# A streaming encoder layer: decay rows without block diagonals, other distances between the steps, and the convolution's pairs in another order

## The chip, the cores and the metric

One Trainium2 chip, one of its cores. The metric is the device time of one execution in microseconds (us), the median of three runs. The engines are TensorE (PE, with its weight loads as PEld), VectorE (DVE), ScalarE (ACT), GpSimd (POOL) and the queue of SyncE (SP), from which the weights are loaded.

## The reference, cut to what matters

One layer of an encoder over 512 prompt frames and 32 further frames of a running stream, all in fp32, with the same weights:

```python
h = rmsnorm(x, g1)
z = h @ w_in                       # 1024 -> 8200 columns, split:
(mq, mk, mv, mo, mi, mf, sb, sc, sx, dq, dk, dv, gt) = jnp.split(z, splits, axis=-1)
# A) mLSTM, 4 heads of 128: per block w = exp(dlog - m), inter = exp(a - m)
s = einsum(q, k) * w
num = einsum(s, v) + inter * einsum(q, C)          # den likewise; C, n carried on
ya = sigmoid(mo) * rmsnorm(num / den, ml_g)
# B) short convolution of width 3
yb = sb * causal_dwconv(sc * sx, hist, sc_w)
# C) differential attention, 4 heads, block-causal mask in chunks of 64
yc = rmsnorm(einsum(softmax(q1 k1) - lam * softmax(q2 k2), v), da_g)
x = x + (sum over branches of sigmoid(gt) * (y_branch @ w_br)) @ w_o
x = x + (silu(conv(up1)) * conv(up2)) @ w_dn       # ConvFFN, width 2816
y = rmsnorm(x, norm_f)
```

The further frames attend to 1024 cached keys as well and start from a given mLSTM state. The outputs are y and the states of both groups.

## The kernel before

Activations stand transposed, channels in the partitions and the 544 frames in the free dimension. Each fp32 product is made of three fp32r matmuls on split operands (high by high, low by high, high by low). The input projection runs over *pairs* of 2 x 128 output columns with a Strassen scheme: seven products ("blocks", `p(pair, w)`, w = 1 to 7) of 4 x 3 = 12 matmuls of 272 columns each, L1677 in `strassen_product`. Other products (branches `pr`, `wo`, `up`, `dn`) are L1645. ACT makes the high part of each weight unit (w_h, L978) and DVE the low part (w_l, L1260), four units ahead of PE; DVE also makes the Strassen weight sums (tw, L1275) and drains three of seven blocks (L1406), ACT the other four (L1093).

All engines run through one list, ORDER, each picking its steps. A planner writes it: `put` and `project` add blocks, and each calls `tick`, a clock that counts one for a block and two for a branch product. `at_time(time, step)` notes a step with its due time, and `tick` puts it into the list once the clock has come to it. So a distance in due times is a distance in blocks of PE. Four chains are placed so:

- The mLSTM, five units u (the 32 further frames first, then four tiles of 128), t0 = 32 + 8u. `s`: PE's decay exponents and scores (L1789 to L1796); `w`: ACT's exponential; `pt`, `qi`: DVE's products (L1464, L1459); `kw`: POOL's product (L845); `n`: PE's numerators (L1809 to L1812), which wait for pt, qi and kw; `rd`, `sq`, `rr`, `hn`: the norm on DVE, ACT, POOL, DVE; `h`: PE's transposes (L1819), which wait for hn; `hm`: ACT's copy; `bd`: POOL's block diagonals for the next unit.
- The decay rows. dlog - m is a column term plus a row term u for each head. The row term and the factor inter are spread over the partitions by one matmul each, with the constant mean_r as stationary operand over 36 rows: `bd_u` and `bd_i` [36, 4, L] hold for each head its row in its own column block, once as high and once (rows 32 to 35) as low part. `block_diagonal` makes them on POOL (L796) from `ui`, which DVE fills in rows step 2.
- The sample group: cached keys (`ck`), then for each of two maps scores (`s`, L1848), maximum (`mx`, DVE) and exponential (`ex`, ACT, L1176).
- Attention, units 1 to 16 (4 heads by 128, 256, 384 and 512 keys), one each 7 due times; unit 0 is the sample group's rest. `s`: scores of both maps (L1862) and the mask (L1867); `mx`; `ex` (L1187); `wd`: DVE's difference of the softmaxes (L1294); `t`: PE's transposes of it (L1882); `wt`; `o` (L1899); `sq`, `rr`, `on`, `y`, `yt`, `yc`: norm and split. The mask adds a product of a row of `causal` (NEG in its first 64 columns) with a row of `mean_r` to the last 64 keys.

The steps that follow a pair (`post`) are due from the clock at which its last block was put: for sx, u0 and u1 (DVE's products of sc and sx, L1534), w0 and w1 (ACT), c0 and c1 (DVE's two sums, L1546 and L1548); for sb, y, hi and lo (L1556, ACT, L1521).

At the start ACT squares the rows of x for the first norm (L955). At the end the last norm needs the sum of squares over the eight column blocks: `mean_square` part 0 over the first seven, part 1 over the last (L1692), then DVE's sum, POOL's power (L912) and the scaling of four prompt chunks and the further frames' rows, each followed by its store.

## Time and profile before

| | us |
|---|---|
| median of 3 runs | 1035.94 (1034.19 to 1041.75) |
| the profiled execution | 1035.7 |
| its span | 1033.9 |
| PE busy | 984.5 |
| DVE busy | 694.6 |
| ACT busy | 462.2 |
| POOL busy | 161.3 |

Durations below come from the one profiled execution; 1.8 us of its time lie outside the span. Matmuls overlap in the pipeline, so the duration of a row with one matmul is longer than the distance to the next start. PEclk is the granted clock of TensorE as a share of 2.4 GHz. "<-" names what a wait ended with; "issue" is a wait for which the profile shows nothing.

### The profile page before, as it was taken

To read this page: it belongs to the slowest core of one execution; us is meant where nothing else is said; L and a number is where in the kernel's file an instruction comes from. 1 tells how busy PE (TensorE), PEld (TensorE's weight loads), DVE (VectorE), ACT (ScalarE), POOL (GpSimd) and SP (SyncE) were. 2 spreads that over 40 slices of the span, in tenths; PEclk is the share of its full clock that TensorE was granted. 3 is DMA by queue.
4 is the path that set the end of the run, shared out by engine and by line. 5 is a ranking of instruction groups with operands and counts; after the bars stand their busy time and mean duration, and the time that the engine had idled before them with its cause. 6 is when DMAs were issued, how large, how long until landed. Compare 5 with 4: busy or idle time off the path is not lost.

```text
span 1033.9 us, 19957 instructions
## 1 busy us (share of the span) xinstructions
PE 984.5 (95%) x7714; PEld 953.9 (92%) x7714; DVE 694.6 (67%) x1176; ACT 462.2 (45%) x965; POOL 161.3 (16%) x348
## 2 busy tenths in 40 slices
PE   6999998998999988899999999999999999999996
PEld 4999887997999987799999999999999999999996
DVE  6887656768666687777787556777777777634342
ACT  5665454465555545555454433433343334322221
POOL 2010222210111111012012211221212121111010
PEclk8999999999999999999999999999999999999998
DMA  6523242364232222232245222222222223423212
...
DMA packets 98069, 96.98 MB, mean 94 GB/s; under 512 B 4740, under 2 KB 93721, under 8 KB 97719
## 3 DMA queue, kind: packets, MB, share of 16 engines
...
## 4 chain that ended last, share of the span: by engine, by line
PE 80%; DVE 9%; ACT 5%; issue 4%; POOL 1%; DMA 0%; ACTq 0%; DVEq 0%; POOLq 0%
PE D L1645 43%; PE D L1677 26%; PE D L1662 2%; DVE w_l L1260 2%; ACT w_h L978 1%; PE X L1862 1%; DVE tw L1275 1%; PE X L1899 1%; DVE ups L1601 1%; DVE acc L1611 1%; PE X L1809 1%; ACT tmp L1150 1%; PE X L1810 1%; PE X L1867 1%; ACT tmp L955 1%
## 5 line engine op out<-in xcount | busy, mean ns | idle before, releaser
L1260 DVE TENSOR_TENSOR w_l<-raw,w_h 128x512 fp32r<-128x512 f32 (+1 forms) x274 | 194.8, 729 | 131.2 <-ACT w_h L978 124.7
L1677 PE MATMUL D<-a_h,w_h 128*128 128x272 f32 x840 | 252.8, 301 | 10.3 <-DVE tmp L1406 5.1
L1677 PE MATMUL D<-a_h,w_l 128*128 128x272 f32 x840 | 245.4, 292 | 0.0
L1677 PE MATMUL D<-a_l,w_h 128*128 128x272 f32 x840 | 244.1, 291 | 0.0
L978 ACT ACTIVATE w_h<-raw 128x512 fp32r<-128x512 f32 (+1 forms) x274 | 163.4, 619 | 105.5 <-PE D L1645 77.2
L1677 PEld LDWEIGHTS D<-a_h,w_h 128*128 128x128 f32 x840 | 160.3, 191 | 15.2 <-DVE tmp L1406 6.5
L1677 PEld LDWEIGHTS D<-a_l,w_h 128*128 128x128 f32 x840 | 160.8, 191 | 0.0
L1677 PEld LDWEIGHTS D<-a_h,w_l 128*128 128x128 f32 x840 | 160.3, 191 | 0.0
L1645 PE MATMUL D<-h_h,w_h 128*128 128x272 f32 x704 | 146.0, 289 | 0.0
L1645 PE MATMUL D<-h_h,w_l 128*128 128x272 f32 x704 | 145.8, 289 | 0.0
L1645 PE MATMUL D<-h_l,w_h 128*128 128x272 f32 x704 | 145.2, 288 | 0.0
L1260 DVE TENSOR_TENSOR w_l<-tw,w_h 128x512 fp32r<-128x512 f32 x120 | 83.9, 707 | 47.0 <-ACT w_h L978 41.5
L1645 PEld LDWEIGHTS D<-h_h,w_h 128*128 128x128 f32 x704 | 110.7, 188 | 0.2
L1645 PEld LDWEIGHTS D<-h_l,w_h 128*128 128x128 f32 x704 | 110.7, 189 | 0.0
L1645 PEld LDWEIGHTS D<-h_h,w_l 128*128 128x128 f32 x704 | 109.9, 189 | 0.0
L1223 ACT ACTIVATE acc<-ups,fcw 128x546 f32<-128x546 f32 x44 | 33.1, 753 | 162.6 <-POOL ffn_last L922 162.6
L978 ACT ACTIVATE w_h<-tw 128x512 fp32r<-128x512 f32 x120 | 75.4, 628 | 67.2 <-PE D L1677 27.0
L1645 PE MATMUL D<-g_h,w_h 128*128 128x272 f32 x352 | 73.4, 290 | 0.7 <-DVE w_l L1260 0.7
L1604 DVE SCALAR_TENSOR_TENSOR acc<-ups,fcw,acc 128x546 f32<-128x546 f32 x44 | 34.7, 788 | 57.8 <-ACT acc L1223 57.8
L1645 PE MATMUL D<-g_l,w_h 128*128 128x272 f32 x352 | 72.8, 288 | 0.0
L1645 PE MATMUL D<-g_h,w_l 128*128 128x272 f32 x352 | 72.7, 288 | 0.0
L1645 PEld LDWEIGHTS D<-g_h,w_h 128*128 128x128 f32 x352 | 55.2, 189 | 1.3 <-DVE w_l L1260 1.0
...
## 6 DMA issues: line engine op xcount, KB each, us to landing
...
xT<-x_spill ACTq DMA_DIRECT2D x1, 2176.0 KB, 11.5
```

Of the source, the lines that this page charges most:

```text
L955: sc.activation(tmp[0:L].rearrange("p a b -> p (a b)")[:, 0:DM], x_t[:, c, :] if c < 4 else x_s[0:TS, :], ACT.Square, accum_out=ssx[0:L, c ...
L978: sc.activation(split_view(w_h, g), whole_view(g), ACT.Copy).then_inc(S["wh_ready"], 1)
L1150: last = sc.activation(ml_junk[0:L, P * h:P * h + P], X[0:L, h // 2, 129 * (h % 2):129 * (h % 2) + P], ACT.Square, scale=rden[0:L, h:h + 1 ...
L1223: sc.activation(acc[part][:, j % 2, 0:T + 2], ups[m % 2][:, 2:T + 4], ACT.Copy, scale=fcw[:, 2, jj:jj + 1])\
L1260: v.tensor_tensor(split_view(w_l, g), whole_view(g), split_view(w_h, g).bitcast(F32), ALU.subtract)\
L1275: v.tensor_tensor(t_view(q, w), x, y, op).then_inc(S["t_ready"], 1)
L1601: last = v.tensor_tensor(to, d, r, ALU.mult)
L1604: link(v.scalar_tensor_tensor(out=ac, in0=u[:, 1:T + 3], scalar=fcw[:, 1, jj:jj + 1], in1=ac, op0=ALU.mult, op1=ALU.add))
L1611: v.scalar_tensor_tensor(out=s[:, 0:T + 2], in0=tmp[:, tmp_row[("up", j)], 0:T + 2], scalar=1.0, in1=s[:, 0:T + 2], op0=ALU.add, op1=ALU.m ...
L1645: last = t.matmul(banks(n)[:, half, 0:HALF], w[:, k, :], x[:, kx + k, HALF * half:HALF * half + HALF], start=kx + k == 0 and i == 0, stop= ...
L1662: last = t.matmul(banks(n)[0:w.shape[2], half, 0:HALF], w[:, k, :], left_of(x, kx)[:, half, :], start=kx == 0 and i == 0, stop=kx == KD - ...
L1677: last = t.matmul(out, wt[:, k, :], x[:, left, k, :], start=w in (1, 2, 5) and k == i == 0, stop=k == KQ - 1 and i == 2, skip_group_check= ...
```

## The change

- Pairs: the convolution's come as sc 0, sx 0, sc 1, sx 1, sb 0, sb 1 (before sc 0, sc 1, sx 0, sx 1, sb 0, sb 1). Its later post steps are due one or two blocks later.
- mLSTM units: every 9 due times (before 8), h at 8.9 (7.9), hm and the state's store at 10 (9). The bd step is gone.
- Decay rows: `sel` is a [4, 4] identity in fp32. For each head one fp32 matmul spreads the row u (added to the causal term) and one the row inter, with a column of sel, repeated, as stationary operand: 4 + 4 matmuls in place of two, without bd_u, bd_i and their POOL and DVE steps. The scores come last.
- Sample group: keys' load due 72 (before 68), transposes 81 and 83 (77, 79), map 0 at 85 to 87 (81 to 83), map 1 at 90 to 92 (84 to 86).
- Attention: starts at 99 (94), the distance to the next unit is 5, 6, 7, 10 after 128, 256, 384, 512 keys (before 7); y, yt and yc keep their distance to the next unit's o.
- Mask: a matrix `late_half` with NEG in row 0 and row 64, so that each map's mask works on its own 64 rows, in fp32; POOL writes it behind the store of C_p.
- Start: ACT squares a constant into `kap` ahead of the first wait for x.
- End: the mean of the first seven blocks (`mean`) and the last one (`norm`) are apart, with the transposes of the last block between; DVE scales chunks 0 to 2, ACT chunk 3 and the further frames' rows.

```diff
-    pairs += [(s, jj) for s in ("sc", "sx", "sb") for jj in range(2)]
+    pairs += [("sc", 0), ("sx", 0), ("sc", 1), ("sx", 1), ("sb", 0), ("sb", 1)]
...
-        t0 = 32 + 8 * u
-        for dt, sub in ((0, "s"), (1, "w"), (1, "qi"), (2, "pt"), (2, "kw"), (3, "bd"), (4, "n"), (5, "rd"), (6, "sq"),
-                        (6, "c"), (6, "rr"), (7, "hn"), (7.9, "h"), (9, "hm")):
-            if sub != "bd" or u < 4:
-                at_time(t0 + dt, "ml", sub, u)
+        t0 = 32 + 9 * u
+        for dt, sub in ((0, "s"), (1, "w"), (1, "qi"), (2, "pt"), (2, "kw"), (4, "n"), (5, "rd"), (6, "sq"),
+                        (6, "c"), (6, "rr"), (7, "hn"), (8.9, "h"), (10, "hm")):
+            at_time(t0 + dt, "ml", sub, u)
         if ML_ORDER[u] >= 3:
-            at_time(t0 + 9, "ml", "out", u)
-    at_time(68, "ck_load")
-    for time, step in ((72, ("ck", 0)), (74, ("ck", 1)), (76, ("sample", "s", 0)), (77, ("sample", "mx", 0)),
-                       (78, ("sample", "ex", 0)), (79, ("sample", "s", 1)), (80, ("sample", "mx", 1)),
-                       (81, ("sample", "ex", 1))):
-        at_time(time + 5, *step)
+            at_time(t0 + 10, "ml", "out", u)
+    at_time(72, "ck_load")
+    for time, step in ((81, ("ck", 0)), (83, ("ck", 1)), (85, ("sample", "s", 0)), (86, ("sample", "mx", 0)),
+                       (87, ("sample", "ex", 0)), (90, ("sample", "s", 1)), (91, ("sample", "mx", 1)),
+                       (92, ("sample", "ex", 1))):
+        at_time(time, *step)
     for u in range(17):
-        t0 = 94 + 7 * (u - 1) - (u == 0)
+        t0, t1 = (99 + 28 * (x // 4) + (0, 5, 11, 18)[x % 4] if x >= 0 else 91 for x in (u - 1, u))
         for dt, sub in ((0, "s"), (1, "mx"), (2, "ex"), (3, "wd"), (5.5, "t"), (6.5, "wt"), (8, "o"), (9, "sq"),
-                        (9, "rr"), (11.5, "on"), (15, "y"), (16, "yt"), (16, "yc")):
+                        (9, "rr"), (11.5, "on"), (t1 - t0 + 8, "y"), (t1 - t0 + 9, "yt"), (t1 - t0 + 9, "yc")):
             if u or dt > 2:
                 at_time(t0 + dt, "at", sub, u)
...
-                                  (1, "sx", "u0"), (2, "sx", "w0"), (3, "sx", "c0"), (3, "sx", "u1"),
-                                  (4, "sx", "w1"), (5, "sx", "c1"), (1, "sb", "y"), (2, "sb", "hi"), (3, "sb", "lo")):
+                                  (1, "sx", "u0"), (2, "sx", "w0"), (3, "sx", "c0"), (5, "sx", "u1"),
+                                  (6, "sx", "w1"), (7, "sx", "c1"), (1, "sb", "y"), (3, "sb", "hi"), (5, "sb", "lo")):
...
+    unit("mean")
+    unit("yT", KD - 1)
     unit("norm", 2)
-    unit("yT", KD - 1)
     unit("scale")
...
+        sel = place("sel", [H, H])
...
+        ui = at(33632, "ui", [H, 2, T])
+        row["u"], row["inter"] = ui[:, 0, :], ui[:, 1, :]
...
+        ml_junk = at(37984, "ml_junk", [P, H * P])
...
+        late_half = at(41472, "late_half", [P, P])
...
+            for c in range(3):
+                sp.wait_ge(S["y_dve"], c + 1)
                 sp.dma_start(y_p[0, P * c:P * c + P, :], yst[:, c, :]).then_inc(S["y_out"], 16)
-            sp.wait_ge(S["y_dve"], 3)
-            sp.dma_start(y_s[0], yst_s[0:TS, :]).then_inc(S["y_out"], 16)
...
-            g.affine_select(out=sel[0:H], in_=sel[0:H], compare_op=ALU.not_equal, fill=float(DM), base=0,
+            g.affine_select(out=sel[:], in_=sel[:], compare_op=ALU.not_equal, fill=1.0, base=0,
                             pattern=[[-1, H]], channel_multiplier=1).then_inc(S["const_ready"], 1)
...
-            def block_diagonal(u):
-                col, L = TILES[ML_ORDER[u]]
-                if u >= 1:
-                    pool.wait_ge(S["ml_scores"], u)
-                for i, out in enumerate((bd_u, bd_i)):
-                    last = g.tensor_tensor(out[:, :, 0:L],
-                                           ui[:, i, col:col + L].bitcast(F32).unsqueeze(1).to_broadcast([36, H, L]),
-                                           sel[:].unsqueeze(2).to_broadcast([36, H, L]), ALU.mult)
-                last.then_inc(S["bd_ready"], 1)
...
-                elif kind == "ml" and a[0] == "bd":
-                    block_diagonal(a[1] + 1)
...
-                    pool.wait_ge(S["ui_ready"], 1)
-                    block_diagonal(0)
...
+                elif kind == "sample" and a == ("ex", 0):
+                    pool.wait_ge(S["out_C"], 64)
+                    link(g.memset(late_half[:], 0.0))
+                    link(g.memset(late_half[0:1, 0:64], NEG))
+                    g.memset(late_half[64:65, 0:64], NEG).then_inc(S["mask_ready"], 1)
+                    pool.wait_ge(S["mask_ready"], 1)
...
+            sc.activation(kap[:], m_half[:], ACT.Square)
...
+                    sc.activation(yst[:, 3, :], yst[:, 3, :], ACT.Copy, scale=ssx[:, 3:4]).then_inc(S["y_act"], 1)
+                    act.wait_ge(S["y_act"], 1)
+                    act.dma_start(y_p[0, 3 * P:4 * P, :], yst[:, 3, :]).then_inc(S["y_out"], 16)
+                    sc.activation(yst_s[0:TS], yst_s[0:TS], ACT.Copy, scale=ssx[0:TS, 4:5]).then_inc(S["y_act"], 1)
+                    act.wait_ge(S["y_act"], 2)
+                    act.dma_start(y_s[0], yst_s[0:TS, :]).then_inc(S["y_out"], 16)
...
-                        .then_inc(S["rows_act"], 1)
+                        .then_inc(S["rows_act"], 2)
...
+
+                    r = 2 if kind == "mean" else a[0]
...
-                    for c in (0, 2):
+                    for c in range(3):
                         v.tensor_scalar(yst[:, c, :], yst[:, c, :], ssx[:, c:c + 1], None, ALU.mult)\
                             .then_inc(S["y_dve"], 1)
-                    v.tensor_scalar(yst_s[0:TS], yst_s[0:TS], ssx[0:TS, 4:5], None, ALU.mult)\
-                        .then_inc(S["y_dve"], 1)
...
-                    dve.wait_ge(S["rows_dve"], 6)
-                    v.memset(ui[:].bitcast(F32), 0.0)
-                    link(v.tensor_copy(sel[32:36], sel[0:H]))
-                elif kind == "rows" and a[0] == 2:
-
-                    dve.wait_ge(S["rows_act"], 2)
-                    v.tensor_copy(ui[0:H, 0, :], row["u"])
-                    link(v.tensor_copy(ui[0:H, 1, :], row["inter"]))
-                    for i, nm in enumerate(("u", "inter")):
-                        last = v.tensor_tensor(ui[32:36, i, :], row[nm], ui[0:H, i, :].bitcast(F32), ALU.subtract)
-                    last.then_inc(S["ui_ready"], 1)
...
-                        B = banks(block_of[("dn", KD - 2)])
-                        wait_drained(pe, block_of[("dn", KD - 2)])
-                        for part in range(2):
-                            mean_square(2, part, B[:, part, 0:5])
+                        mean_square(2, 1, banks(block_of[("dn", KD - 2)])[:, 1, 0:5])
+                elif kind == "mean":
+                    wait_drained(pe, block_of[("dn", KD - 2)])
+                    mean_square(2, 0, banks(block_of[("dn", KD - 2)])[:, 0, 0:5])
...
+                            pe.wait_ge(S["rows_act"], 3)
                             for i in range(4, 8):
                                 wait_drained(pe, last_user[i])
                         else:
                             pe.wait_ge(S["ml_c"], u)
 
-                        pe.wait_ge(S["bd_ready"], u + 1)
-                        lw, inter = (X[:, i, :].rearrange("p (h t) -> p h t", h=H)[:, :, 0:L] for i in (0, 2))
+                        lw = X[:, 0, :].rearrange("p (h t) -> p h t", h=H)[:, :, 0:L]
                         t.matmul(lw[0:L], ident_r[0:L, 0:L], causal[0:L, 0:L].unsqueeze(1).to_broadcast([L, H, L]),
                                  start=True, stop=False, skip_group_check=True)
-                        t.matmul(lw[0:L], mean_r[0:36, 0:L], bd_u[:, :, 0:L], start=False, stop=True,
-                                 skip_group_check=True)
                         for h in hs:
-                            t.matmul(X[0:L, 1, P * h:P * h + L], mkT[:, h, col:col + L], mqT[:, h, col:col + L],
+                            t.matmul(X[0:L, 0, P * h:P * h + L], sel[:, h:h + 1].to_broadcast([H, L]), row["u"][:, col:col + L],
+                                     start=False, stop=True, skip_group_check=True)
+                        for h in hs:
+                            t.matmul(X[:, 2, P * h:P * h + L], sel[:, h:h + 1].to_broadcast([H, P]), row["inter"][:, col:col + L],
                                      start=True, stop=True)
-                        t.matmul(inter, mean_r[0:36, :], bd_i[:, :, 0:L], start=True, stop=True)\
-                            .then_inc(S["ml_scores"], 1)
+                        for h in hs:
+                            last = t.matmul(X[0:L, 1, P * h:P * h + L], mkT[:, h, col:col + L],
+                                            mqT[:, h, col:col + L], start=True, stop=True)
+                        last.then_inc(S["ml_scores"], 1)
...
+                            pe.wait_ge(S["mask_ready"], 1)
...
+                            d = slice(64 * c, 64 * c + 64)
+                            last = t.matmul(X[:, c, nk - 64:nk], late_half[d, :], mean_w[d, 0:64], start=False,
                                             stop=True, skip_group_check=True)
                         last.then_inc(S["at_s"], 1)
```

## Rows read from the trace of the kernel before

**Rows 1.** The page, busy time: engine, us (share of the span), instructions.
```profile
PE 984.5 (95%) x7714; PEld 953.9 (92%) x7714; DVE 694.6 (67%) x1176; ACT 462.2 (45%) x965; POOL 161.3 (16%) x348
```

**Rows 2.** Waits of PE, whole span: us in total, times, longest.
```profile
PE X L1882 <- DVE prob L1294: 5.7, 4, 1.9
PE X L1819 <- DVE qi L1487: 5.6, 5, 1.4
...
PE D L1677 <- DVE tmp L1406: 5.1, 6, 1.2
...
PE X L1809 <- issue: 3.0, 1, 3.0
PE X L1848 <- ACT prob L1176: 2.1, 1, 2.1
...
PE D L1677 <- ACT tmp L1093: 1.5, 3, 1.0
```

**Rows 3.** Windows: stretch, length; busy of PE, PEld, DVE, ACT, POOL; PEclk; DMA; GB/s.
```profile
118.00:236.00 118.00, 107.23 (x814) 100.25 (x813) 77.19 (x145) 59.28 (x163) 27.44 (x37) 0.97 0.41 112
330.00:440.00 110.00, 98.90 (x710) 91.34 (x709) 83.33 (x162) 59.68 (x149) 14.62 (x43) 0.95 0.25 68
440.00:560.00 120.00, 119.39 (x938) 116.95 (x937) 89.97 (x146) 65.39 (x140) 18.43 (x32) 1.00 0.32 95
```

**Rows 4.** Windows of two short stretches, columns as in rows 3.
```profile
118.30:119.50 1.20, 1.20 (x6) 1.14 (x6) 0.00 (x0) 0.00 (x0) 0.00 (x0) 0.50 0.05 14
162.00:165.20 3.20, 3.12 (x14) 3.15 (x15) 3.20 (x6) 0.50 (x1) 0.00 (x0) 0.50 0.00 0
```

**Rows 5.** Timeline of PE, scores of unit 1: start, us, engine, line, operation.
```profile
128.24 0.49 PE L1791 MATMUL X<-bd_u,mean_w 36*128 36x512 f32 x1
128.66 1.16 PE L1794 MATMUL X<-mqT,mkT 128*128 128x128 f32 x8
129.75 0.50 PE L1796 MATMUL X<-bd_i,mean_w 36*128 36x512 f32 x1
```

**Rows 6.** Timeline of PE, the first tile's kw products.
```profile
116.94 1.50 PE L1812 MATMUL X<-mv_tok,kw 32*128 32x129 f32 x8
```

**Rows 7.** Timeline of DVE and POOL ahead of unit 2's numerators.
```profile
157.00 4.03 DVE L1275 TENSOR_TENSOR tw<-raw,tw 128x512 f32<-128x512 f32 x1
...
158.44 1.04 POOL L796 TENSOR_TENSOR bd_u<-ui,sel 36x512 fp32r<-36x512 f32 x1
...
161.31 0.67 DVE L1464 TENSOR_TENSOR p_ml<-w_ml,X 128x512 f32<-128x512 f32 x1
```

**Rows 8.** Timeline of DVE and PE around the transposes of attention unit 9.
```profile
375.96 0.78 DVE L1546 SCALAR_TENSOR_TENSOR scb<-u_c,vec,scb 128x546 f32<-128x546 f32 x1
...
377.62 0.65 DVE L1534 TENSOR_TENSOR u_c<-tmp,scb 128x480 f32<-128x480 f32 x1
...
378.96 0.35 DVE L1294 SCALAR_TENSOR_TENSOR prob<-prob,kap 128x128 f32<-128x128 f32 x1
...
379.37 0.33 PE L1882 MATMUL X<-ident,prob 128*128 128x128 f32 x1 [1.59 <-DVE prob L1294]
```

**Rows 9.** Timeline of PE, scores and mask of attention unit 8.
```profile
352.46 1.13 PE L1862 MATMUL X<-dkT,dqT 64*128 64x512 f32 x4
...
353.52 0.41 PE L1867 MATMUL X<-mean_w,causal 1*128 1x64 f32 x2
```

**Rows 10.** Timeline of ACT and PE at the start.
```profile
5.08 1.28 ACT L955 ACT_TABLE_LOAD   x1 [5.08 <-DMA x_t<-in_x_prompt]
...
13.74 0.41 PE L1698 MATMUL X<-diag,mean_w 32*128 32x32 f32 x2 [0.28 <-DVE diag L1327]
```

**Rows 11.** Timeline of PE at the end.
```profile
1022.27 1.21 PE L1692 MATMUL D<-mean_w,tmp 128*128 128x1 f32 x10
...
1023.40 0.66 PE L1919 MATMUL X<-ident,xT 128*128 128x128 f32 x4
```

**Rows 12.** The chain that ended last: one block of 12 matmuls, start and us.
```profile
111.10 1.51 PE D L1677 x12
```

38 lines of the change are left out of this document (13 added, 25 removed).

## The prediction

> **What bounds the kernel now.** I read the page's busy line first: TensorE (PE) is busy 984.5 us, 95% of the span [rows 1]. A change that leaves PE's own work alone can give back only PE's idle stretches and the time at the lower clock. So I asked the waits of PE next [rows 2], and a table by stage to see where they lie [rows 3]. From 118 to 236 us (the mLSTM units) PE idles 118 - 107.23 = 10.8 us; from 330 to 440 us (the short convolution with attention) 110 - 98.90 = 11.1 us; from 440 to 560 us, with the same attention but no convolution, only 0.6 us. The reader is to see in that table also the granted clock, 0.97 and 0.95 of full where PE idles, 1.00 where it doesn't. Short windows show the two levels: 0.50 (1.2 GHz) from 118.3 and from 162.0 us [rows 4]; the second follows an idle of 3 us [rows 2], the first no idle but matmuls with few rows or columns, those of [rows 6] last. At half clock a stretch costs half its length.
>
> **Decay rows (PE work added).** A full unit loses two fp32r matmuls over 512 columns, which start 0.42 us (128.24 to 128.66) and some 0.43 us ahead of what follows: 0.85 us [rows 5]. It gains eight fp32 matmuls of 4 rows by 128 columns, each two passes: 16 passes. The nearest passes of that width with 128 rows are the scores, eight passes in 1.09 us, 0.136 us each [rows 5]; the nearest with few rows are those with kw of the first tile, eight in about 1.45 us (1.50 with their drain), 0.18 us each, part of it at half clock [rows 6]. The mask's one-row passes are worse still: 0.17 us for 64 columns, and 64 more columns are an eighth of a 512-column pass, 0.53 / 8 = 0.07: 0.24 us [rows 9]. Bounds: 16 x 0.136 - 0.85 = +1.3 us and 16 x 0.24 - 0.85 = +3.0 us a unit. I take 0.155 us, close to the kw row less what is clock in it, since those are fp32 passes in a run of their own as the new ones are: 16 x 0.155 - 0.85 = +1.63 us, four units +6.5 us. The first tile has 32 columns; its price lies between 0 and that of a full unit, I take +1.0. Sum +7.5 us, bounds +5.2 and +13.5.
>
> The Trainium skill speaks against the change here. "TensorE: Matmul & The Clock Gate", Part 3, says a weight load overlaps a running matmul only when its row group differs, and its LDWEIGHTS section gives 128 columns as 128/1.2 = 107 ns. By it each pass is a load and then a stream of about the same length, 0.21 us, an estimate that would make the item some 12 us; the trace has no pass of 4 rows by 128 columns to say so.
>
> **Clock behind them.** The half clock from 118.3 us came after matmuls that fill little of the array [rows 4, 6]. A unit now has 2.5 us of 4-row matmuls ahead of its scores. A stretch at half clock costs half its length, about 1 us for one of the size of that from 118.3 to 121 us. Bounds 0 and five of them; I take one: +1.0 us.
>
> **Spacing 9 and h later.** The transposes of h wait five times for hn, 5.6 us in all, 1.4 at most [rows 2]. Step h now stands one more block (1.51 us of PE work [rows 12]) behind hn, and a block covers the longest of them: -5.6 us. The 3.0 us wait in front of unit 2's numerators [rows 2] is one of DVE: a tw sum that begins at 157.00 lasts 4.03 us while POOL runs kw, bd_u and bd_i, so p_ml ends only at 162.0 [rows 7]. The two bd products a unit (1.04 us each) are removed, and kw stands three blocks behind the store that it followed directly. Both go: -3.0 us, and with it the half clock from 162.0 to 165.2, half of 3.2 = -1.5 us [rows 4]. Sum -10.1 us. If a wait of about 1 us comes up between tok drains and the shifted units, -9.
>
> **Sample group.** The second scores wait 2.1 us for the first exponential [rows 2], three blocks after the first scores; they now stand five blocks after. -2.1 us. PE's 1.5 us for ACT's tmp drains comes while ACT waits for a maximum in the same stretch; the distance from maximum to exponential is unchanged, so I take half: -0.8 us. Bounds for both together: 0 and -3.6.
>
> The first attention output (o of unit 0) moves from ahead of pr(0, 0) to behind it in the order, and DVE, which must wait for at_o before it drains pr(0, 0), is held for as long as PE takes for a group of transposes, a block and o. PE has four split units (6 us) in hand and needs that drain only for pr(0, 1), which stands behind o, s and one more block. Nothing, or +1 us if DVE catches up late.
>
> **Mask.** Per unit two one-row fp32r matmuls over 64 columns take 0.34 us between starts (0.41 with their drain) [rows 9]. Their successors have two passes each, but lie in different row halves. If the halves overlap, as two maps of 512 columns in 1.06 us suggest [rows 9] (four passes, each four times the columns of a 0.136 us pass, would be 2.2 one after the other), the price is the same; if not it is up to 0.15 us more. 16 units: I take -0.3, bounds -2 and +2.4 us.
>
> **Convolution order and spacing.** DVE did two conv sums c0 (the first at 375.96, 0.78 us each) and the product u1 (0.65 us and small ones) between the exponential and the softmax difference (378.96); PE's transpose waits from 377.8 to 379.37 [rows 8]. The same pattern stands at units 9 to 12: prob 5.7 us in four waits, the drains that come late after them 5.1 us in six [rows 2], and stretches at half clock behind three of them. The table's 0.95 over 110 us caps that loss at 5.5 us [rows 3]; ten matmuls at double interval in each make it 3. In the new order sx 0 stands one pair (7 blocks) earlier, u1 and c1 two blocks later, y, hi and lo are spread, and attention takes 5, 6, 7, 10 blocks for 128 to 512 keys rather than 7 each. By the due times, unit 9's difference then has only u0 ahead of it, unit 10's only u1. So the waits should go. But DVE is full: 83.3 us in this stretch [rows 3], where PE without idle and slow clock needs 110 - 11.1 - 3 = 96 us: it would have to be busy 87% of it, in order and without a wait that PE feels. I count on two thirds of 11.1 + 3 = 14.1 us: -9 us, bounds -3 and -13.
>
> **Start and end.** ACT's table load (1.28 us at 5.08, behind the first data) moves ahead of the data, but PE waits only 0.28 us for the last diag that depends on it [rows 10]; DVE's copies hold the rest. -0.4 us, bounds 0 and -1.3. At the end the last column block's transposes (0.7 us) move ahead of the last mean square, which ran 1022.27 to 1023.40 [rows 11]; POOL's power and both scalings follow 0.7 us later, and the DVE now has three chunks. The store of y_s is shorter than the chunk issued last before, which gives a little back. +0.7 us, bounds -0.5 and +1.5.
>
> **Sum.** +7.5 + 1.0 - 10.1 - 2.9 - 0.3 - 9.0 - 0.4 + 0.7 = -13.5 us. The profiled execution took 1035.7 us (span 1033.9 and 1.8 around it), the median of three is 1035.94: 1035.7 - 13.5 = 1022.2, say 1022 us.
>
> **Rivals.**
> (A) DVE's load, not its order, bounds the convolution: the idle moves by 7 blocks and shrinks by 2 to 3 us only. For it: 83.3 us busy with PE stalled. Against: DVE idles 110 - 83.3 = 26.7 us of the same stretch. 1022 + 6.5 = 1028.5 us. Chance 0.17.
> (B) In the 4-row passes weight load and stream don't overlap: 0.18 to 0.24 us a pass, by the kw and the mask rows, +9.5 to +13.5 for the item, in the middle +11.5: 1026 us. For it: both rows have few array rows. Against: part of the one is half clock, the other is fp32r between streams of another shape. 0.20. This is what the page's rule above would make.
> (C) Slower: the eight 4-row matmuls a unit lower the clock and it doesn't come back between units. Place: the five units. Work at half clock takes twice its time. The units span 5 x 9 blocks of 1.51 us, 68 us of work; with a fifth of it (13.5 us) at half clock the gain is gone, with half of it the time is 1022 + 34 = 1056 us. For it: [rows 4]'s fall without idle. Against: the blocks between the units gave the clock back there before the next unit. 0.05.
> (D) The change's waits do go but come up elsewhere in attention, where two units now stand only five blocks apart (on, rr and o): +5, 1027 us. 0.08.
> Forecast, with its neighbours: 0.50.
>
> **From this to the numbers.** About 1% (10.4 us) is what a measurement of this kernel tells from no change, so faster means below 1025.6. Forecast wholly, half of B and a little of D fall there: 0.50 + 0.10 + 0.02 = 0.62. Slower (above 1046.3, C with a third of the work): 0.03 of C, and 0.02 for what I don't see. Same: 0.33. Range: the gains at their bounds (-10.1, -3.6, -2, -13, -1.3, -0.5) with +5.2 give 1010 us; two thirds of the way there from 1022 is 1014, and at the other end A with B, 1022 + 6.5 + 4, gives 1032.
>
> **What would show it.** Right: no PE wait on qi or at the numerators of unit 2; no bd on POOL; the wait at the second sample scores gone; the four waits on prob L1294 below 2 us together; eight sel matmuls in 2.3 to 2.7 us a unit; the clock at 1.00 behind them. Wrong: sel passes at 0.2 us or more, the clock at 0.5 after each unit (C), or the waits for tmp L1406 and prob still near 10 us (A).

## The result, and the profile after

The changed kernel takes 1012.6 us, median of four runs (1012.49 to 1012.78); the kernel before, run beside it, 1036.8 (1034.19 to 1041.75). The ratio is 0.9761, 95% interval 0.9724 to 0.9799: 2.4% faster, 24.2 us. The forecast was 1022 us, range 1014 to 1032. The direction was right; the gain was 24 us where 13.5 had been worked out, and the time lies below the range.

The profiled execution has a span of 1011.0 us. The busy line of its page, and then PE's waits, which answer to [rows 1, 2]:

```profile
PE 980.3 (97%) x7816; PEld 959.4 (95%) x7816; DVE 684.7 (68%) x1170; ACT 464.0 (46%) x966; POOL 161.3 (16%) x341
...
PE D L1702 <- DMA x_t<-in_x_prompt: 5.1, 1, 5.1
PE D L1643 <- DVE a_l L1327: 4.7, 5, 3.2
PE X L1891 <- ACT wdT L1190: 2.8, 2, 2.0
...
PE X L1793 <- issue: 0.9, 1, 0.9
...
PE D L1658 <- DVE tmp L1398: 0.3, 1, 0.3
...
PE X L1868 <- DVE prob L1286: 0.2, 1, 0.2
```

Lines have moved: the blocks' L1677 is L1658 now, the numerators' L1809 is L1793, the probabilities' transposes L1882 are L1868. Gone are the five waits for qi (5.6 us) and that of the second sample scores (2.1); the waits for prob fell from 5.7 to 0.2 us and those for tmp L1406 from 5.1 to 0.3. New are two for ACT's wdT, 2.8 us in all. The table by stage, cut where [rows 3] cuts it (us; busy time of PE, its loads, DVE, ACT, POOL; granted clock, DMA share, GB/s):

```profile
118.00:236.00 118.00, 114.91 (x905) 110.80 (x904) 77.86 (x154) 63.91 (x170) 22.15 (x34) 0.97 0.42 111
...
330.00:440.00 110.00, 106.67 (x830) 102.33 (x829) 94.53 (x182) 67.44 (x169) 25.81 (x53) 0.98 0.27 78
440.00:560.00 120.00, 119.14 (x946) 117.78 (x946) 85.14 (x131) 61.13 (x119) 20.59 (x29) 1.00 0.36 112
```

The mLSTM's idle fell from 10.8 to 3.1 us and that of the convolution's stretch from 11.1 to 3.3. The third row shows 0.9 us of idle, where [rows 3] had 0.6: nothing was to be had there, and nothing came.

For a whole account I cut both PE timelines at three starts that exist in both: the first mLSTM scores, the first transposes of ck, the first product with yc. From the first to the last of these, with the same number of blocks between, before took 410.9 us and after 389.1: 21.7 us of the 22.9 by which the spans differ. 18.3 us of it are idle rows (25.6 to 7.3). The matmuls of the blocks around a wait took 0.15 us more than their pitch for each wait that went, some 2 us. The new decay rows added 4.7 us, the new mask took 2.7, and 3 us are half clock. Ahead of the first scores 0.8 us went, behind the first product with yc 0.4.

### The profile page after: what moved, and what is told of

It reads as the page before. It is cut to its first block, busy times and chain, and to the rows that moved or that the text cites. A ratio compares the mean times of both kernels' runs of the same rounds, so it can differ in the third digit from the quotient of the medians.

```text
span 1011.0 us, 20145 instructions
## 1 busy us (share of the span) xinstructions
PE 980.3 (97%) x7816; PEld 959.4 (95%) x7816; DVE 684.7 (68%) x1170; ACT 464.0 (46%) x966; POOL 161.3 (16%) x341
## 4 chain that ended last, share of the span: by engine, by line
PE 82%; DVE 7%; ACT 4%; issue 4%; DMA 1%; POOL 1%; ACTq 0%; DVEq 0%; POOLq 0%; SPq 0%
PE D L1626 43%; PE D L1658 28%; PE D L1643 3%; DVE w_l L1252 2%; ACT w_h L969 1%; PE X L1847 1%; PE X L1885 1%; DMA x_t<-in_x_prompt 1%; DVE acc L1592 1%; DVE ups L1582 1%; PE X L1779 1%; PE D L1743 1%; PE X L1793 1%; DVE f_x L1331 0%; PE X L1794 0%
## 5 line engine op out<-in xcount | busy, mean ns | idle before, releaser
L1658 PE MATMUL D<-a_h,w_h 128*128 128x272 f32 x840 | 251.8, 300 | 3.4 <-ACT mqT L1085 1.5
L1658 PE MATMUL D<-a_h,w_l 128*128 128x272 f32 x840 | 244.4, 291 | 0.0
L1658 PE MATMUL D<-a_l,w_h 128*128 128x272 f32 x840 | 243.2, 290 | 0.0
L1658 PEld LDWEIGHTS D<-a_h,w_h 128*128 128x128 f32 x840 | 159.8, 190 | 6.1 <-ACT mqT L1085 1.7
L1658 PEld LDWEIGHTS D<-a_l,w_h 128*128 128x128 f32 x840 | 160.1, 191 | 0.0
L1658 PEld LDWEIGHTS D<-a_h,w_l 128*128 128x128 f32 x840 | 159.5, 190 | 0.0
L1085 ACT ACTIVATE tmp<-D 128x272 f32<-128x272 f32 x72 | 28.5, 396 | 65.1 <-PE D L1658 53.4
```

What stands on the lines that cost most here:

```text
L1085: sc.activation(dst_of(q, blk, half), chain_bank(q, w), ACT.Copy, scale=scale_of(q))\
L1658: last = t.matmul(out, wt[:, k, :], x[:, left, k, :], start=w in (1, 2, 5) and k == i == 0, stop=k == KQ - 1 and i == 2, skip_group_check= ...
```

## The experiments

Each kernel is the changed one with the edit shown, unless another is named. Times are medians of four runs, with the ratio to the kernel before on the same chip. That kernel's own median moved between 1034 and 1039 us, which is in every ratio, while the changed kernel's four runs lie within 0.3 us and the stages below repeat from run to run. So I compare two kernels by their times and stages, and say so where their ratios' intervals overlap. "mLSTM" is the stage from the first mLSTM scores to the first transposes of ck, "attention" the one from there to the first product with yc, both from the profiled execution. Within kernels of one mLSTM code the first varies by 1.8 us with the stretches at half clock of that execution; the second repeats to 0.2 us where its code is the same.

| kernel | us | ratio, 95% | mLSTM | attention |
|---|---|---|---|---|
| changed | 1012.6 | 0.976 (0.972 to 0.980) | 118.8 | 270.3 |
| old_rows | 1011.3 | 0.972 (0.970 to 0.975) | 116.5 | 270.3 |
| old_rows_bd5 | 1010.7 | 0.975 (0.973 to 0.978) | 116.5 | 270.3 |
| rows_128 | 1009.3 | 0.975 (0.972 to 0.977) | 114.2 | 270.3 |
| old_mask | 1014.9 | 0.976 (0.974 to 0.978) | 118.8 | 272.5 |
| mask_c1_first | 1012.5 | 0.977 (0.975 to 0.980) | 117.3 | 270.5 |
| mask_one_row | 1014.4 | 0.979 (0.977 to 0.981) | 117.3 | 272.8 |
| old_ml_gaps | 1025.2 | 0.986 (0.983 to 0.989) | 129.8 | 271.2 |
| old_order | 1016.7 | 0.978 (0.976 to 0.980) | 118.8 | 274.0 |
| old_posts | 1013.4 | 0.976 (0.973 to 0.979) | 118.8 | 270.2 |
| even_att | 1014.8 | 0.978 (0.974 to 0.982) | 118.8 | 273.1 |
| old_conv | 1012.5 | 0.975 (0.972 to 0.979) | 117.0 | 270.3 |
| old_conv_100 | 1012.1 | 0.976 (0.973 to 0.978) | 118.7 | 269.8 |
| old_conv_101 | 1024.1 | 0.987 (0.985 to 0.990) | 118.8 | 282.0 |
| new_conv_101 | 1020.3 | 0.984 (0.981 to 0.986) | 118.8 | 278.0 |
| u1_at_4 | 1011.5 | 0.975 (0.972 to 0.978) | 117.3 | 269.9 |
| rows_128_u4 | 1008.4 | 0.973 (0.970 to 0.976) | 115.7 | 269.7 |

Beside them stands before_at_99, the kernel before with one number changed: 1024.6 us, ratio 0.987 (0.984 to 0.990), stages 115.6 and 286.2 us. The kernel before itself has 116.5 and 294.4; it has four blocks fewer in the first stage and four more in the second.

### The convolution: order, offsets, gaps

My forecast gave 9 us to three edits: the pairs' order, the later offsets of u1, w1, c1, hi and lo, and the uneven gaps of attention. Undone one at a time:

```diff
-    pairs += [("sc", 0), ("sx", 0), ("sc", 1), ("sx", 1), ("sb", 0), ("sb", 1)]
+    pairs += [(s, jj) for s in ("sc", "sx", "sb") for jj in range(2)]
```

> The changed kernel with the convolution's pairs back in the order C0 C1 x0 x1 B0 B1, all else as changed. Theory A: the order carries the convolution's gain (about 11 us: 6.9 of idle, the tails of those waits, the half clock): 1020 us or more, with waits on prob and tmp of 6 us or more in all. Rival B: the later u1, c1, hi and lo and the uneven gaps of attention carry it, the order only moves DVE's load: 1012 to 1015 us.

3.7 us more in its stage (1016.7 us): between the two theories, less than half of what the order was to carry. The waits for prob didn't return; one of 4.9 us for wdT came.

```diff
-                                  (1, "sx", "u0"), (2, "sx", "w0"), (3, "sx", "c0"), (5, "sx", "u1"),
-                                  (6, "sx", "w1"), (7, "sx", "c1"), (1, "sb", "y"), (3, "sb", "hi"), (5, "sb", "lo")):
+                                  (1, "sx", "u0"), (2, "sx", "w0"), (3, "sx", "c0"), (3, "sx", "u1"),
+                                  (4, "sx", "w1"), (5, "sx", "c1"), (1, "sb", "y"), (2, "sb", "hi"), (3, "sb", "lo")):
```

> The changed kernel with the old offsets alone: u1, w1, c1 at 3, 4, 5 blocks behind a pair rather than 5, 6, 7, and hi, lo of the B pairs at 2, 3 rather than 3, 5. Theory A: since the order alone gave back only 3.8 us, the offsets carry about as much: +3 to +5 us, 1016 to 1018 us, with u1 again between exponential and softmax difference. Rival B: with the new order u1 at 5 is itself late: the one long wait of the changed kernel (PE 1.95 us at 380.91, where ACT had waited 3.43 us for the u1 product) goes, with the 1.5 us of half clock behind it: -3 us, 1009.5 us.

Nothing: 270.2 us against 270.3. The long wait for wdT is shorter (three waits, 1.6 us in all), and waits for prob and tmp of the same length take its place. Both theories missed.

```diff
-        t0, t1 = (99 + 28 * (x // 4) + (0, 5, 11, 18)[x % 4] if x >= 0 else 91 for x in (u - 1, u))
+        t0, t1 = (99 + 28 * (x // 4) + (0, 7, 14, 21)[x % 4] if x >= 0 else 91 for x in (u - 1, u))
```

> The changed kernel with seven steps for every attention unit again rather than 5, 6, 7 and 10 for 128 to 512 keys. Theory A: the gaps carry a third of the convolution's gain, since a unit of 512 keys with its longer exponential, difference and eight transposes has only seven blocks: +3 us, 1016 us. Rival B: the gaps matter for nothing while PE finds other blocks: 0 to +1 us.

2.7 us more, as theory A had it. So far the edits seem to be worth 6 us. All three undone together:

> The changed kernel with all three of the convolution's edits undone together (pair order, offsets of u1, w1, c1, hi and lo, and seven steps for each attention unit); new rows, new mask and new mLSTM spacing stay. Theory A: the three together carry the whole difference in idle of that stretch (11.1 us before, 4.2 after), the tails of those waits and the clock: +9 to +11 us, 1022 to 1024 us, with four waits on prob of 5 us in all. Rival B: part of the idle of before came from the mLSTM stage or the mask and won't return: +4 to +6 us, 1017 to 1019 us (the order alone gave back 3.8).

It costs nothing: 1012.5 us, and its attention stage takes 270.3 us as in the changed kernel. Both theories fall. Each edit matters only given the others; as a set they are worth nothing here. What then took the idle of before away? With the three undone, one difference to the kernel before is left in that stretch, and it is one that I had not listed among its causes: the attention units start at step 99 instead of 94. Units and convolution pairs both come every seven blocks, so 99 is two blocks earlier against the pairs than 94 + 7 = 101. Three kernels move only this. The first is old_conv with

```diff
-        t0, t1 = (99 + 28 * (x // 4) + (0, 7, 14, 21)[x % 4] if x >= 0 else 91 for x in (u - 1, u))
+        t0, t1 = (101 + 28 * (x // 4) + (0, 7, 14, 21)[x % 4] if x >= 0 else 91 for x in (u - 1, u))
```

> The kernel old_conv (all three convolution edits undone, which cost nothing: its stage from the first attention scores to the first product with yc took 232.10 us, as in the changed kernel) with the attention units two steps later, at 101 + 7x rather than 99 + 7x. The changed kernel's list starts them at 99 and the one of before at 94, and 94 + 7 = 101, so this is the old phase between attention units and convolution pairs, which also come every seven blocks. Theory A: the waits of before were a matter of this phase: the waits on prob and tmp come back, +8 to +12 us, about 1022 us. Rival B: the phase is nothing, the idle went with the new mLSTM spacing, rows or mask (clock, DVE's backlog): 1012 to 1014 us.

11.7 us more in the stage, 1024.1 us: theory A. Two lines of its PE waits, near those of the kernel before (5.7 us in four and 5.1 in six, [rows 2]), and its stretch from 330 to 440 us:

```profile
PE X L1868 <- DVE prob L1286: 6.1, 4, 2.5
...
PE D L1658 <- DVE tmp L1398: 4.1, 5, 1.2
```

```profile
330.00:440.00 110.00, 99.71 (x729) 93.43 (x728) 82.96 (x162) 61.15 (x154) 14.18 (x45) 0.94 0.26 73
```

The reader sees [rows 3] again: 10.3 us idle, 0.94 of the clock. Of the 11.7 us only 4.6 are idle rows (10.2 us in this stage, 5.5 in old_conv); most of the rest is the clock, at half for 13.7 us of the stage and in old_conv for none. One step later than 99 is harmless (100, 269.8 us), two steps cost all:

> old_conv with the attention units one step later (100 + 7x). Theory A (phase): between the two, +3 to +6 us over old_conv's 1012.5, more waits on prob than at 99 and fewer than at 101. Rival B: no change, 1012.5 us within 1 us.

So the loss doesn't grow with the distance, as my theory A had it for this kernel; it sets in between 100 and 101 (rival B for 100). The converse, in the kernel before:

```diff
-        t0 = 94 + 7 * (u - 1) - (u == 0)
+        t0 = 99 + 7 * (u - 1) - (u == 0)
```

> The kernel before with one number changed: the attention units start at step 99 instead of 94, so two steps earlier against the convolution pairs in a period of seven (94 + 7 = 101). Nothing of the change's order, offsets, gaps, rows or mask. Theory A (phase): the 11.1 us of idle between 330 and 440 us fall to 3 to 5 us, with the half clock behind three waits: 1036 - 10 = 1026 us. Rival B (the gain came from other parts): within 2 us of 1036.

12.7 us faster by the medians, by this one number: theory A. Its four executions lie between 1022.7 and 1027.7 us and the profiled one is the slowest; against the profile of before its span is 8.1 us shorter and its attention stage 8.2. Of its profile, the same stretch, and DVE's rows around the softmax difference of a unit:

```profile
330.00:440.00 110.00, 108.13 (x828) 102.49 (x829) 93.29 (x184) 69.33 (x178) 25.87 (x53) 1.00 0.30 82
```

```profile
372.21 0.75 DVE L1294 SCALAR_TENSOR_TENSOR prob<-prob,kap 128x512 f32<-128x512 f32 x1
...
375.29 0.78 DVE L1546 SCALAR_TENSOR_TENSOR scb<-u_c,vec,scb 128x546 f32<-128x546 f32 x1
376.11 0.79 DVE L1548 SCALAR_TENSOR_TENSOR scb<-u_c,vec,scb 128x546 f32<-128x546 f32 x1
376.94 0.65 DVE L1534 TENSOR_TENSOR u_c<-tmp,scb 128x480 f32<-128x480 f32 x1
```

The difference (here of a unit of 512 keys) stands ahead of the two sums and the product u1, where in [rows 8], at a unit of 128 keys, it stood behind them. In the stretch there are 1.9 us idle where 11.1 had been, full clock, and no row for DVE's prob among its PE waits; the waits for qi, for the second sample scores and the 3.0 us are all still there, so it is the convolution's part alone. Some 3 us of idle came up elsewhere in the stage (0.9 us at 319.6, 0.9 at 464.1 and 1.2 at 478.8 us), so the idle of the whole stage fell by 6.0 us, from 14.8 to 8.8, and not by 9.2. And the three edits in the bad phase:

> The changed kernel, all its convolution edits kept, with the attention units two steps later (101 rather than 99). Theory A: the phase is what counts for the old order too, and the new order, offsets and gaps were made for where they stand: in this phase they save part of what the old ones lose there, 1016 to 1019 us. Rival B: the edits make the stretch insensitive to the phase: 1012.6 us within 1 us. Rival C: they do nothing against the phase, as much idle as the old ones there: 1022 us.

There they save 4.0 of the 11.7 us: theory A. They are a remedy for a phase that the kernel no longer has.

### The spacing of the mLSTM units

```diff
-        t0 = 32 + 9 * u
+        t0 = 32 + 8 * u
...
-                        (6, "c"), (6, "rr"), (7, "hn"), (8.9, "h"), (10, "hm")):
+                        (6, "c"), (6, "rr"), (7, "hn"), (7.9, "h"), (9, "hm")):
```

> The changed kernel with the mLSTM units eight steps apart again and h at 7.9, hm at 9, rows and all else as changed. Theory A: the spacing alone took the five waits for qi: they return with 5.6 us, and each costs some 0.16 us more than its idle row shows: +6.4 us, 1019 us. Rival B: with no bd products on POOL the vector engines are early enough by themselves: waits for qi of 0.5 us or less each, +2 us or less, 1014.5 us.

12.6 us slower by the medians, about 10 by the ratios (the four executions lie between 1023.2 and 1027.2 us, and the profiled one is 1026.7); its mLSTM stage is 11.0 us longer. The idle is theory A's, the price is nearly twice its +6.4. The waits return to the tenth:

```profile
PE X L1803 <- DVE qi L1468: 5.6, 5, 1.4
```

That is 5.3 us of idle in all, and as much again in matmuls that run longer: the blocks of the stage 3.1 us, the decay rows and scores 2.3. Most of this is the clock. The stage here, and then in the kernel before, which has the same five waits but the old decay rows:

```profile
106.00:235.80 129.80, 121.38 (x904) 115.32 (x903) 73.56 (x152) 61.81 (x173) 21.46 (x32) 0.93 0.38 92
```

```profile
106.00:222.50 116.50, 105.73 (x787) 98.09 (x787) 75.23 (x146) 57.72 (x166) 31.41 (x40) 0.97 0.36 98
```

At half clock are 17.1 us of the stage here, and 6.8 us both in the changed kernel and in the one before. So the short waits cost about twice their idle rows in this execution, together with the passes over 4 rows; in the kernel before the same waits did not.

### The decay rows

Here the rows alone go back to their old form (two fp32r matmuls of 512 columns over 36 rows; POOL's `block_diagonal`, DVE's splitting), under the new spacing:

> The changed kernel with the decay rows alone put back as they were (block-diagonal products on POOL, two fp32r matmuls of 512 columns a unit, DVE's splitting of the rows), all spacing as changed. Theory A, from the two traces' steps: the new rows cost PE 4.8 us of matmuls (a full unit's four groups take 3.30 us where they took 2.35) and some 2.7 us at half clock behind the scores of units 1 and 3; against it stand 0.7 us of a wait at 66 us. So without them 1012.6 - 4.8 - 2.7 + 0.7 = about 1006 us. Rival B: the bd products on POOL and the row work on DVE were what stalled unit 2 for 3.0 us and, with its half clock, cost 4.7 us, so their return takes back nearly all of that: 1010 to 1012 us, with the wait at the numerators of unit 2 there again. Price as forecast (C): 7.5 + 1.0 us, 1004 us.

1.3 us less by the medians, 1.7 by the spans: rival B, and the new rows are a small net cost at most, since the ratios' intervals overlap. By stage: 0.7 us is gained ahead of the first scores, where DVE no longer splits the rows and PE no longer waits at 66 us, and 2.3 are lost behind (0.5 against the executions of the same mLSTM code with one stretch at half clock fewer, 117.0 us). A wait of 2.9 us at numerators is back although the spacing is new, at unit 1 where the kernel before had it at unit 2. Its cause shows in a pair of rows from DVE and POOL. With the old rows (the kernel with bd two steps later, below):

```profile
136.16 3.93 DVE L1283 TENSOR_TENSOR tw<-raw,tw 128x512 f32<-128x512 f32 x1
...
136.50 1.06 POOL L845 TENSOR_TENSOR kw<-mk_tok,w_ml 128x512 f32<-128x512 f32 x1
137.50 1.04 POOL L796 TENSOR_TENSOR bd_u<-ui,sel 36x512 fp32r<-36x512 f32 x1
138.50 1.04 POOL L796 TENSOR_TENSOR bd_i<-ui,sel 36x512 fp32r<-36x512 f32 x1
```

With the new rows:

```profile
136.43 0.75 POOL L853 DMA_DIRECT2D out<-k_out  x1 [9.64 <-ACT k_out L1049]
137.18 0.54 POOL L855 DMA_DIRECT2D out<-k_out  x1
137.40 1.95 DVE L1267 TENSOR_TENSOR tw<-raw,tw 128x512 f32<-128x512 f32 x1
137.73 1.06 POOL L833 TENSOR_TENSOR kw<-mk_tok,w_ml 128x512 f32<-128x512 f32 x1
```

DVE's sum, 0.68 us where POOL is idle, ends 0.6 us behind POOL's last product in both and lasts 2.0 us less where two of the three products (2.1 us) are gone. By the Trainium skill ("SBUF — State Buffer", "SBUF: two separate sides") DVE with two SBUF inputs and a GpSimd instruction that reads SBUF exclude each other at a shared port pair, and whichever starts first has it for its whole instruction. The rows agree that the two exclude each other. They do not show that order: DVE's sum starts 0.3 us ahead of POOL's first product in both (POOL's times are rough in a profile) and is the one that is held, and it gets no turn between the three products. An attempt to keep the old rows and move the products away, in old_rows:

```diff
-        for dt, sub in ((0, "s"), (1, "w"), (1, "qi"), (2, "pt"), (2, "kw"), (3, "bd"), (4, "n"), (5, "rd"), (6, "sq"),
+        for dt, sub in ((0, "s"), (1, "w"), (1, "qi"), (2, "pt"), (2, "kw"), (4, "n"), (5, "bd"), (5, "rd"), (6, "sq"),
```

> The kernel old_rows (changed spacing, order and mask, decay rows as before), but the block-diagonal products two steps later on POOL: at 5 behind the scores rather than 3. In old_rows PE waited 2.9 us for unit 1's numerators and ran them at half clock; DVE's products of that time (1.52 and 1.08 us where 0.68 is usual) stood beside the two bd products. Theory A: the bd products beside DVE's work ahead of the numerators cost it: the 2.9 us wait falls to 1 us, with 1.5 us of half clock, and the time to 1011.3 - 3.4 = about 1008 us, the fastest so far; the old rows are then the better form. Rival B: the wait isn't bd's (the changed kernel without bd has 0.9 us of it), or it moves to the scores, which then wait for bd: 1010 to 1012 us.

The wait stayed at 2.9 us and the stage at 116.5: rival B by the time, but the pair of rows above is from this kernel and shows why it doesn't clear bd: POOL was late itself, behind its DMA issues, so that its three products ran back to back at either due time. The move that was to part them didn't.

Does the small number of rows matter? `ui` and `sel` were filled with zeros to 128 rows, so that the same sixteen passes contract over 128:

```diff
-        sel = place("sel", [H, H])
+        sel = place("sel", [P, H])
...
-        ui = at(33632, "ui", [H, 2, T])
-        row["u"], row["inter"] = ui[:, 0, :], ui[:, 1, :]
+        ui = at(33632, "ui", [P, 2, T])
+        row["u"], row["inter"] = ui[0:H, 0, :], ui[0:H, 1, :]
...
+                    link(v.memset(ui[:], 0.0))
...
-                            t.matmul(X[0:L, 0, P * h:P * h + L], sel[:, h:h + 1].to_broadcast([H, L]), row["u"][:, col:col + L],
+                            t.matmul(X[0:L, 0, P * h:P * h + L], sel[:, h:h + 1].to_broadcast([P, L]), ui[:, 0, col:col + L],
...
-                            t.matmul(X[:, 2, P * h:P * h + L], sel[:, h:h + 1].to_broadcast([H, P]), row["inter"][:, col:col + L],
+                            t.matmul(X[:, 2, P * h:P * h + L], sel[:, h:h + 1].to_broadcast([P, P]), ui[:, 1, col:col + L],
```

> The changed kernel, but the selector and the two decay rows filled up with zeros to 128 rows, so that the sixteen passes of a unit contract over 128 rows and not over 4. Theory A: the number of rows is nothing to a pass's price (0.124 us with 4 rows, the scores' 0.115 to 0.136 with 128), and a stretch at half clock behind the scores of one or two units stays, since it comes of short matmuls in a row: 1012 to 1014 us, 2.0 us of sel matmuls a unit. Rival B: few rows is what lowers the clock there: no stretch at double interval behind the scores, 2.5 us less, 1010 us. Rival C: a pass over 4 rows has its price because so little is loaded; with 128 rows it rises to the 0.136 us: 16 x 4.5 x 0.012 = +0.9 us.

3 to 4.6 us less in the stage than with 4 rows (a second kernel with 128 rows, rows_128_u4, below, has 1.3 to 3.1 less): rival B, and the opposite of rival C. By the medians it is 3.3 us, with ratios' intervals that overlap. Unit 3, with 4 rows and then with 128 (start, us, engine, line, x passes; a row of eight passes is four matmuls of two):

```profile
173.93 0.48 PE L1770 MATMUL X<-causal,ident 128*128 128x512 f32 x1
174.34 1.15 PE L1773 MATMUL X<-ui,sel 4*128 4x128 f32 x8
175.33 1.05 PE L1776 MATMUL X<-ui,sel 4*128 4x128 f32 x8
176.31 1.37 PE L1779 MATMUL X<-mqT,mkT 128*128 128x128 f32 x8
```

```profile
171.75 0.48 PE L1771 MATMUL X<-causal,ident 128*128 128x512 f32 x1
172.07 1.05 PE L1774 MATMUL X<-ui,sel 128*128 128x128 f32 x8
172.95 1.06 PE L1777 MATMUL X<-ui,sel 128*128 128x128 f32 x8
173.85 1.06 PE L1780 MATMUL X<-mqT,mkT 128*128 128x128 f32 x8
```

From start to start the sixteen sel passes take 1.97 us with 4 rows and 1.78 with 128. But the single pass costs the same: inside the run the starts lie 0.112 us apart in both kernels, so that part of theory A holds. With 4 rows the first pass alone takes 0.21 us and the last 0.20, so the first eight take 0.99 (0.88 with 128 rows) and the second eight 0.98 (0.90). Their neighbours pay too: causal to sel 0.41 and 0.32 us, and the scores of a unit without half clock 0.92 and 0.81. So there is a charge of about 0.1 us on both sides of each change between 128 rows and 4, 0.39 us a unit, 1.6 of the 3 or more; the rest is the clock. Windows behind the scores of units 1 and 3 of the changed kernel (the first runs on into a block):

```profile
129.20:132.70 3.50, 3.50 (x17) 3.50 (x18) 0.00 (x0) 0.86 (x2) 0.00 (x0) 0.52 1.21 85
177.70:180.40 2.70, 2.70 (x13) 2.70 (x13) 0.76 (x2) 1.14 (x4) 1.04 (x1) 0.50 0.51 166
```

PE did not idle there (3.50 of 3.50 us) and ran at 1.2 GHz, right behind the unit's sixteen passes over 4 rows, from its scores on. All 13 profiled kernels with 4-row selectors have such a stretch from the scores of unit 1 on, 12 of them without a PE wait in the 20 us before it (old_ml_gaps has one of 1.2 us); the two with 128 rows and the two with the old rows under the new spacing have none there. The 4-row passes are not its only cause: the kernel before has no such stretch at unit 1, but before_at_99, whose code is the same up to there, has one of 6.8 us, from 0.3 us into its scores on, behind a wait of 1.19 us and one matmul over 36 rows:

```profile
127.40:134.20 6.80, 6.80 (x30) 6.14 (x29) 1.26 (x3) 1.55 (x8) 0.00 (x0) 0.50 0.97 116
```

The whole stage with 128 rows:

```profile
105.00:240.00 135.00, 131.91 (x1083) 126.03 (x1085) 92.28 (x178) 75.60 (x195) 22.63 (x35) 1.00 0.43 117
```

### The mask

```diff
-                            last = t.matmul(X[:, c, nk - 64:nk], late_half[d, :], mean_w[d, 0:64], start=False,
+                            last = t.matmul(X[:, c, nk - 64:nk], causal[64:65, :], mean_r[64:65, 0:64], start=False,
```

> The changed kernel with the attention mask alone as it was: a pair of one-row fp32r matmuls over 64 columns a unit. Theory A: the trace's 0.26 us for the four passes instead of 0.34, and 0.10 us less for the scores ahead of them (0.96 instead of 1.06 at 512 columns), both come from the mask: 16 x 0.18 = +2.9 us, 1015.5 us. Rival B: the scores are shorter for another reason: 16 x 0.08 = +1.3 us, 1013.9 us. Rival C, my forecast's: +0.3 us, 1012.9 us.

2.1 us more in the stage. Of the same unit (512 keys) with the old mask, and with the new one:

```profile
347.17 1.13 PE L1847 MATMUL X<-dkT,dqT 64*128 64x512 f32 x4
348.23 0.41 PE L1852 MATMUL X<-mean_w,causal 1*128 1x64 f32 x2
```

```profile
345.85 1.13 PE L1847 MATMUL X<-dkT,dqT 64*128 64x512 f32 x4
346.82 0.33 PE L1853 MATMUL X<-mean_w,late_half 64*128 64x64 f32 x4
```

The mask starts 0.97 us behind the scores rather than 1.06, and what follows starts 0.26 us behind it rather than 0.33: theory A's two parts, 2.7 us over 16 units (1.6 and 1.1). The stage shows 0.6 less: the blocks ran 0.9 us shorter, without the half clock behind the wait for wdT, and PE idled 0.3 more. Three causes are possible: row halves, type, number of rows. The first kernel swaps the mask's two matmuls and leaves the scores, the second takes one row of each half.

```diff
-                        for c in range(2):
+                        for c in (1, 0):
```

> The changed kernel with the two mask matmuls of a unit in the other order, so that the first uses the same row half (64 to 127) as the last scores ahead of it and the second the other half. Theory A: the scores lost 0.10 us a unit and the mask 0.08 because neighbours lie in different row halves and overlap; then the first mask matmul gives that 0.1 us back: +0.08 to +0.10 us for 16 units, 1014 us, and the maps of 512 columns take 1.02 to 1.06 us again. Rival B: the gain comes of the fp32 type, next to fp32 scores, instead of a change to fp32r and back: no change, maps 0.96 us, mask 0.26 us.

```diff
-                            d = slice(64 * c, 64 * c + 64)
+                            d = slice(64 * c, 64 * c + 1)
```

> The changed kernel with mask matmuls over one row each (rows 0 and 64) rather than 64, fp32 as before it. Theory A: the rows are nothing, type and row half are what counts: maps 0.96 us and mask 0.26 us as in the changed kernel, 1012.6 us within 1 us. Rival B: a one-row matmul can't overlap its neighbours, as the old one-row ones seemed not to: maps 1.06 and mask 0.34 us, +2.5 us.

The order of the halves is nothing (0.97 and 0.26 us again, 1012.5 us): rival B by the time, though not by its reason, the type, as the next kernel shows. One row in place of 64, in fp32 still, costs all and a little more:

```profile
345.58 1.13 PE L1847 MATMUL X<-dkT,dqT 64*128 64x512 f32 x4
346.64 0.44 PE L1853 MATMUL X<-mean_w,late_half 1*128 1x64 f32 x4
```

1.06 us to the mask and 0.36 behind it: 2.5 us more in the stage, rival B. It is the number of rows, or rather that it changes from 64 to 1 and back. The Trainium skill ("TensorEngine Tiling (Array Packing)", "Key Properties") states that changing the tiling mode, not just the tile, drains the TensorE. If a change of the row count is such a change of mode, and the other half only another tile, the rows agree, here and for the decay rows: 0.07 to 0.11 us at each change of the count, nothing for the other half.

### A faster version

The longest new wait of the changed kernel is PE's 1.95 us at 380.91 for wdT. ACT's copy stood behind its drain of a tmp pair, which had waited 3.43 us for DVE's u1 product. u1 a block earlier:

```diff
-                                  (1, "sx", "u0"), (2, "sx", "w0"), (3, "sx", "c0"), (5, "sx", "u1"),
-                                  (6, "sx", "w1"), (7, "sx", "c1"), (1, "sb", "y"), (3, "sb", "hi"), (5, "sb", "lo")):
+                                  (1, "sx", "u0"), (2, "sx", "w0"), (3, "sx", "c0"), (4, "sx", "u1"),
+                                  (5, "sx", "w1"), (7, "sx", "c1"), (1, "sb", "y"), (3, "sb", "hi"), (5, "sb", "lo")):
```

> The changed kernel with u1 of the x pairs at 4 and w1 at 5 blocks rather than 5 and 6. Theory A: the wait at 380.91 comes from ACT, whose drain of the next pair's tmp stands 3.43 us behind the u1 product with the copy of wdT behind it in ACT's queue; u1 a block (1.5 us) earlier takes most of the 1.95 us and the 1.5 us of half clock that follow: -3 us, 1009.6 us. Rival B: DVE is late by its load, u1 only pushes what stands behind it (the maximum of the next unit): the wait moves and the time stays within 1 us.

That wait fell to 0.98 us and one for tmp of 1.10 came up: 0.4 us in the stage, rival B. Together with the 128 rows:

> Two findings put together: decay rows and selector filled with zeros to 128 rows (rows_128: 1009.3 us, no half clock in the mLSTM stage), and u1, w1 of the x pairs at 4 and 5 blocks (u1_at_4: 1011.5 us, the wait of 1.95 us at one unit's transposes down to 0.98, others 1.1 us longer; its stage took 231.7 us instead of 232.1). Theory A: they touch different stages and add, 1009.3 - 0.4 = about 1009 us, at most 1 us less. Rival B: the wait at that unit, without which the clock also stays up, gives 1.5 us more: 1007.5 us.

1008.4 us, ratio 0.973 (0.970 to 0.976), the lowest time of all; the step from rows_128 lies within the intervals, and the time is between the two theories. It had a stretch at half clock behind the first tile's kw matmuls (32 rows), and none behind any scores.

## Why the prediction was wrong

**Decay rows: +7.5 forecast, +4.7 measured, below its low bound of +5.2.** The price per pass was the wrong shape: I took 0.155 us for each of sixteen, and inside the run a pass over 4 rows takes 0.112 us, as over 128; the few rows cost about 0.1 us at each change of the row count instead (0.124 us a pass with those inside the run). The row I leaned to (kw of the first tile, 0.18) was half clock in the main: the same eight matmuls take 1.08 us in the changed kernel, 0.135 each. And the low bound missed a part: the scores next to the 36-row matmuls had paid for their neighbourhood (1.09 us, 0.92 now), so the unit gains 0.17 us that I didn't count. My upper bound was a slip besides: four units at 3.0 and a first tile up to 3.0 are 15, not 13.5. The Trainium skill's rule that I set against the change ("TensorE: Matmul & The Clock Gate", Part 3: load and stream one after the other, 0.21 us) isn't borne out at 0.112 us a pass: rival B is false.

**Clock behind them: +1.0 forecast.** Right in kind and too small: 1.3 to 3.1 us, measured against rows_128.

**Spacing: -10.1 forecast, near it in the two traces.** The waits for qi are gone (-5.6), and that of 3.0 us at unit 2's numerators with the half clock behind it (1.7). One of 0.9 us came at unit 1's numerators: I had kw three blocks behind the store of k_out that it followed directly, and it follows it directly there too (136.43 to 137.73 above), beside DVE's sum, which it holds by 1.3 us. bd was what had stretched that sum to 4.03 us [rows 7]. What I didn't see is that this term and the decay rows aren't independent: with the new rows, going back to the old spacing costs 11 us in the stage for waits of 5.6, nearly half of it clock.

**Sample group: -2.9 forecast, -3.7 measured.** The second scores' 2.1 us went, and all of ACT's tmp drains (1.3 us) and a DVE drain of 0.3 rather than half. In before_at_99, which leaves the group's spacing alone, both stand as before. No run undoes this spacing by itself, nor the edits at the start and the end, so these two terms rest on the waits and intervals of the two traces.

**Mask: -0.3 forecast, -2.7 in its rows and -2.1 when undone alone, beyond its low bound of -2.** I asked whether the four passes overlap by row halves. The price was elsewhere, at the change from 64 rows to one and back, which the rows of before couldn't show apart [rows 9].

**Convolution: -9 forecast.** The stretch from 330 to 440 us gave 7.8 us of idle, and the phase alone is worth 11.7 us of its stage in old_conv and 8.2 in the kernel before, with the clock. So the size was near by luck, and the reason was false. The step that failed is that the new order and offsets would clear DVE's queue between exponential and difference. They are worth nothing as a set at the new start, and 4.0 us at the old one. The start of attention, 94 to 99, stood in the diff; I had used it for the first output (o of unit 0) and never for the phase. [rows 8] shows the collision itself rightly, two sums and a product ahead of the difference; what removed it was the difference coming two blocks earlier, ahead of them. Rival A (DVE's load as the bound) is refuted by the same rows: before_at_99 has DVE busy 93.3 of 110 us and PE idle 1.9.

**Start and end: +0.3 forecast in sum, about -1 measured.** 0.1 us at the first product, and 0.7 from a place I hadn't named, the splitting of the rows on DVE. From the issue of the last product to the end it is 13.4 us against 13.55: POOL's power comes 0.34 us later, and the shorter last store gives back 0.5.

Rivals C and D: the clock did fall behind the units, but for 3 us and not 13; a wait did come up in attention, 2.0 us for wdT.

The errors by term, forecast less measured: decay rows 2.8, mask 2.4, convolution about 2, start and end 1.3, sample 0.8, against 0.3 to 2.1 the other way for the clock behind the rows. The two profiled executions differ by 22.9 us and not 13.5, so the miss is 9.4 us; the blocks around the waits that went, some 2 us, are in no term. Nearly all errors have one sign. I had shaded each gain towards nothing and each cost upwards, and treated the half clock as a separate small item, when idle and short passes bring it together.
